# Modulation products summed in batches with one turn for each, and some of them moved to other places of the program

## The reference

```python
m_lat = jnp.split(s_lat @ w_ada[li] + b_ada[li], 6, axis=-1)     # s_lat = silu(c)
m_ctx = jnp.split(s_ctx @ w_ada[li] + b_ada[li], 6, axis=-1)
h = rms_norm(x, g_mix[li]) * (1.0 + m_lat[1]) + m_lat[0]
p = h @ w_in[li]                       # 9 x 256 columns: Fourier, attention, gMLP parts
...
x = x + m_lat[2] * (y @ w_out[li])
h = rms_norm(x, g_ffn[li]) * (1.0 + m_lat[4]) + m_lat[3]
x = x + m_lat[5] * conv_ffn(h, ffn_up[li], ffn_conv[li], ffn_conv_b[li], ffn_down[li])
```

## Time and profile before

| | |
|---|---|
| runs | 3271.11, 3277.59, 3277.39 us; median 3277.39 |
| profiled execution | 3273.77 us, of it the span of the trace 3272.0 us |
| PE busy | 3098.2 us (95%) |
| DVE, ACT, GpSimd busy | 1319.4, 742.9, 542.3 us |
| modulation chunks (line 229), PE busy | 114.0 us |
| loaded from HBM | 334.26 MB, 102 GB/s over the span |

### The profile page before, as it was taken

How to read it: one execution, slowest core, us unless ns; L and a number is a source line. 1 busy time by engine, 2 the same in 40 slices (tenths; PEclk the granted TensorE clock), 3 DMA queues, 4 the chain that set the end, 5 groups by cost and what they waited for, 6 DMA issues and landing times.

```text
span 3272.0 us, 39252 instructions
## 1 busy us (share of the span) xinstructions
PE 3098.2 (95%) x15593; PEld 2342.5 (72%) x15593; DVE 1319.4 (40%) x2198; ACT 742.9 (23%) x1413; POOL 542.3 (17%) x445
## 2 busy tenths in 40 slices
PE   7989999999989899999979999999999998999999
PEld 4546478888655788644469888844488887698888
DVE  1045368772224343255456656532245322223100
ACT  2034121110123231134234444421000001221100
POOL 1000035554100000000022222100145442011000
PEclk9989999999998999999989999999999998999999
DMA  6228412222316443334300000121222223211343
GB/s 238 77 77 319 183 65 90 91 91 90 103 64 252 148 154 141 141 130 166 142 7 14 14 14 14 46 90 65 77 78 88 80 90 107 90 40 43 148 144 116
DMA packets 51808, 337.66 MB, mean 103 GB/s; under 512 B 6304, under 2 KB 7968, under 8 KB 12608
## 3 DMA queue, kind: packets, MB, share of 16 engines
q1 hardware_dynamic: 47088, 323.05, 27.4%
q10 hardware_dynamic: 2976, 7.14, 0.6%
q0 software_dynamic: 1584, 5.21, 0.5%
HBM read 334.26 MB, written 1.11 MB: 102 GB/s over the span
## 4 chain that ended last, share of the span: by engine, by line
PE 83%; issue 9%; ACT 4%; DVE 2%; DVEq 0%; ACTq 0%; DMA 0%; POOL 0%; POOLq 0%
PE psum L208 29%; PE psum L2482 24%; PE psum L229 3%; PE psum L304 3%; PE psum L1425 3%; PE psum L1407 2%; PE psum L2051 2%; PE psum L371 2%; PE psum L242 1%; PE psum L1416 1%; ACT h_sb L887 1%; PE psum L398 1%; ACT arena L1680 1%; PE psum L1463 1%; PE psum L1486 1%
## 5 line engine op out<-in xcount | busy, mean ns | idle before, releaser
L208 PE MATMUL psum<-h_sb,ring 128*128 128x256 f32 (+1 forms) x2560 | 792.0, 470 | 16.5 <-ACT h_sb L887 16.4
L208 PEld LDWEIGHTS psum<-h_sb,ring 128*128 128x128 f32 x2560 | 484.9, 191 | 312.6 <-issue 266.3
L208 PE MATMUL psum<-arena,ring 128*128 128x256 f32 (+1 forms) x1504 | 418.1, 442 | 16.9 <-DVEq L716 7.5
L208 PEld LDWEIGHTS psum<-arena,ring 128*128 128x128 f32 x1504 | 291.9, 194 | 144.1 <-issue 92.5
L2482 PE MATMUL psum<-arena,ring 128*128 128x256 f32 x1168 | 267.4, 379 | 0.0
L2482 PEld LDWEIGHTS psum<-arena,ring 128*128 128x128 f32 x1168 | 221.9, 190 | 30.2
L2482 PE MATMUL psum<-h_sb,ring 128*128 128x256 f32 x912 | 216.6, 387 | 8.6 <-ACT h_sb L887 8.5
L2482 PE MATMUL psum<-arena,c 128*128 128x256 f32 x888 | 205.2, 379 | 1.8 <-DVE arena L2520 1.2
L1730 POOL TENSOR_TENSOR ring<-c,gates 128x512 f32<-128x512 f32 x32 | 32.6, 1041 | 1026.9 <-PE psum L208 797.2
L2482 PEld LDWEIGHTS psum<-h_sb,ring 128*128 128x128 f32 x912 | 174.2, 193 | 39.8 <-ACT h_sb L887 8.6
L2482 PEld LDWEIGHTS psum<-arena,c 128*128 128x128 f32 x888 | 168.5, 190 | 25.8 <-DVE arena L2520 2.0
(11 more groups left out here) (311 smaller groups left out, 4240.9 us busy)
## 6 DMA issues: line engine op xcount, KB each, us to landing
ring<-in_stream SPq DMA_DIRECT2D x302, 1024.0 KB, 4.8
arena<-decays SPq DMA_DIRECT2D x24, 256.0 KB, 3.6
x_sb<-in_x ACTq DMA_DIRECT2D x1, 2048.0 KB, 17.5
arena<-in_rpb POOLq DMA_DIRECT2D x32, 64.0 KB, 5.3
arena<-in_c POOLq DMA_DIRECT2D x1, 1120.0 KB, 7.9
x_sb<-in_ctx ACTq DMA_DIRECT2D x1, 1024.0 KB, 7.0
c<-in_c ACTq DMA_DIRECT2D x1, 1024.0 KB, 4.9
out<-x_sb POOLq DMA_DIRECT2D x1, 1024.0 KB, 5.0
```

The lines of the kernel that those rows point to most:

```text
L208: ins = pe.matmul(out_ap, lhs(k), rhs(k), start=first and k == 0, stop=last and k == nk - 1)
```

## The change

- **Batches.** `ADA_BATCHES` cuts the 96 chunks into nine batches of 4 to 16. The stationary operand is now a window of 32 columns in a wider `silu_w` (992 columns in all) whose place depends on the chunk's number q in its batch, so that its two rows land at 2q and 2q+1 of each group of 32. All chunks of a batch accumulate in the same 256 columns of bank 7; ACT copies once for a batch, behind its last chunk, and PE turns once, with a wider `sel`. A turn stands ahead of the first chunk of the next batch, or at the end of four parts (`TURNED_AT_END`).
- **Places.** Of the 40 chunks of attention 0, 16 go into the first projection (two behind each of its first eight chunks) and 2 into the gap behind layer 0's output projection (`gap1`). Attention 1 keeps 17; 4 go into the gap behind layer 0's feed-forward stage (`gap2`), 3 behind layer 1's output projection (`gap3`), 4 behind its feed-forward stage (`gap4`); the layer 2 projection keeps 20. `GAP_AHEAD` says how many of a gap's chunks stand ahead of the norm's products on PE. The stream follows.
- **ACT.** `act_norm` copies the batch that ends in a gap before its table load and Ln. It waits for the modulation only behind the Exp. In layers 2 and 3 the norm now stands ahead of the loads of constants.
- **Start.** ACT loads `c` alone first (16 KB), then `ident`, the rest of `vec`, `ones`, `x`. PE no longer waits for all of them. The first norm's squares are added on DVE, so PE has two sum products instead of eight, behind the eight chunks.
- **Others.** The gains of layer 1 are made in the feed-forward stage of layer 0, and its second item waits for them; the two sets of GpSimd's sum buffers are swapped, and its second chunk there waits for the fourth turn.

```diff
+QKV_TURNS = 8
+QKV_ADA = [3] * 4 + [2] * 4
+ADA_PARTS = _spans([("ada_first", MIX_ADA), ("ada_in1", 16), ("ada_next0", 22), ("gap1", 2), ("gap2", 4),
+                    ("ada_next1", 17), ("gap3", 3), ("gap4", 4), ("ada_last", sum(QKV_ADA))])
+GAP_AHEAD = {"gap1": 2, "gap2": 0, "gap3": 1, "gap4": 2}
+ADA_BATCHES = [(0, 8), (8, 24), (24, 36), (36, 48), (48, 52), (52, 62), (62, 72), (72, 84), (84, 96)]
+TURNED_AT_END = ("ada_first", "gap1", "gap3", "ada_last")
...
         def pe_ada(pe, name, i):
 
             n, a = ada_at(name, i)
-            if a == 0:
-                pe.wait_ge(S["silu_ready"], 1)
-            elif i > 0:
-                pe_turn(pe, a - 1)
+            batch, q, last = ada_batch(a)
+            if a > 0 and q == 0 and a not in [ADA_PARTS[part][1] for part in TURNED_AT_END]:
+                pe_turn(pe, batch - 1)
             arrived(pe, n)
             for half in range(2):
                 for j in range(4):
                     k = 4 * half + j
-                    ins = pe.matmul(bank(7)[32 * j:32 * (j + 1), 0:256], silu[:, a // (2 * ADA_CHUNKS), k, :],
-                                    w[:, n % RING, k, :], start=half == 0, stop=half == 1)
+                    ins = pe.matmul(bank(7)[32 * j:32 * (j + 1), 0:256],
+                                    silu[:, a // (2 * ADA_CHUNKS), k, ADA_ROWS - 2 - 2 * q:2 * ADA_ROWS - 2 - 2 * q],
+                                    w[:, n % RING, k, :], start=q == 0 and half == 0, stop=last and half == 1)
                 ins.then_inc(S["products"], 1)
...
+        def pe_ada_first(pe):
+            pe.wait_ge(S["silu_ready"], 1)
+            for i in range(MIX_ADA):
+                pe_ada(pe, "ada_first", i)
+            pe_norm_sums(pe, 0, TOK)
+            pe.wait_ge(S["silu_ready"], 2)
+            pe_turn(pe, 0)
...
         def pe_norm_sums(pe, k, cols):
 
-            added = KT + 2 * k - 1
+            gap = f"gap{k}"
+            if gap in ADA_PARTS:
+                for i in range(GAP_AHEAD[gap]):
+                    pe_ada(pe, gap, i)
+            added = 2 * k + 1
             pe.wait_ge(S["n_sq"], added)
...
+            if gap in ADA_PARTS:
+                for i in range(GAP_AHEAD[gap], ada_count(gap)):
+                    pe_ada(pe, gap, i)
+                if gap in TURNED_AT_END:
+                    pe_turn(pe, ada_batch(ADA_PARTS[gap][1] - 1)[0])
...
+                if li == 0 and c < IN1_CHUNKS - 1:
+                    for i in range(2):
+                        pe_ada(pe, "ada_in1", 2 * c + i)
...
-        def act_norm(act, use, l, part, norm=None, streams=2):
+        def act_norm(act, use, l, part, norm=None, streams=2, mods=None):
+            if f"gap{norm}" in ADA_PARTS:
+                act_ada_all(act, f"gap{norm}")
 
             if norm is not None:
                 act_log_exp_set(act)
                 act.wait_ge(S["n_sum"], norm + 1)
                 act_rsqrt(act, rinv[:, 0:streams * SEQ], bank(5)[:, 0:streams * SEQ], 1.0 / D).then_inc(S["n_rinv"], 1)
+            if mods is not None:
+                act.wait_ge(S["mods_ready"], mods)
...
-            act.dma_start(vec[:, :], t["vec"]).then_inc(S["loaded_vec"], 16)
+            act.dma_start(vec[:, 0:4 * KT], t["vec"][:, 0:4 * KT]).then_inc(S["loaded_c"], 16)
             act.dma_start(ident[:, :], t["ident"]).then_inc(S["loaded_vec"], 16)
+            act.dma_start(vec[:, 4 * KT:], t["vec"][:, 4 * KT:]).then_inc(S["loaded_vec"], 16)
             act.dma_start(ones[:, :], t["ones"]).then_inc(S["loaded_vec"], 16)
...
-            dve_squares(dve)
+            for kt in range(KT):
+                dve_square(dve, kt, 2)
...
+        b["act_norm"](act, 4, 2, 0, 4, mods=4)
         act.wait_ge(T["arena_free"], 1)
         act.dma_start(self.c2[:, 0:CD["end"]], t["c_delta"]).then_inc(T["loaded_c2"], 16)
...
-            act.wait_ge(S["mods_ready"], 4)
+            act.wait_ge(S["mods_ready"], 5)
+            b["act_norm"](act, 6, 3, 0, 6)
             act.wait_ge(T["arena_free"], 2)
```

More of the change, by code:

```diff
@@ L51, in _offsets, with _spans @@
     return out
+def _spans(counts):
+    at, out = 0, {}
+    for name, count in counts:
+        out[name] = (at, at + count)
+        at += count
+    return out
 VEC_SIZES = [("c", 4 * KT)]
@@ L173, in build_program, with ada_count @@
         sched = {}
+        def ada_count(name):
+            first, end = ADA_PARTS[name]
+            return end - first
         def plan(name, chunks, results):
@@ L209, in k_products, with in1_chunk, qkv_chunk, qkv_turn @@
             ins.then_inc(S["products"], 1)
+        def in1_chunk(li, c):
+            return sched[f"1in{li}"][0] + (3 * c if li == 0 else c)
+        def qkv_chunk(c):
+            return sched["2qkv"][0] + c + sum(QKV_ADA[:c // 2]) + c % 2
+        def qkv_turn(i):
+            return [i < sum(QKV_ADA[:j + 1]) for j in range(QKV_TURNS)].index(True)
         def ada_at(name, i):
             first, end = ADA_PARTS[name]
+            if name == "ada_in1":
+                return in1_chunk(0, i // 2) + 1 + i % 2, first + i
             if name == "ada_last":
-                return sched["2qkv"][0] + 5 * (i // 3) + (1, 3, 4)[i % 3], first + i
+                j = qkv_turn(i)
+                r = i - sum(QKV_ADA[:j])
+                return qkv_chunk(2 * j + (r > 0)) + 1 + (r > 1), first + i
             return sched[name][0] + i, first + i
@@ L236, in turned, with pe_turn @@
             return bank(7)[:, at + 2 * m0:at + 2 * m1]
-        def pe_turn(pe, a):
-            pe.wait_ge(S["ada_copied"], a + 1)
-            l, c = divmod(a, ADA_CHUNKS)
+        def pe_turn(pe, batch):
+            pe.wait_ge(S["ada_copied"], batch + 1)
+            first, end = ADA_BATCHES[batch]
+            l, c = divmod(first, ADA_CHUNKS)
+            cols = turned(l, 2 * c, 2 * (c + end - first)).rearrange("p (q m s) -> p m q s", m=2, s=2)
             for m in range(2):
-                ins = pe.matmul(turned(l, 2 * c + m, 2 * c + m + 1), rows[:, 256 * (a % 2) + 128 * m:256 * (a % 2) + 128 * (m + 1)],
-                                sel[:, :], start=True, stop=True)
+                at = 256 * (batch % 2) + 128 * m
+                ins = pe.matmul(cols[:, m], rows[:, at:at + 128],
+                                sel[:, 0:2 * (end - first)].rearrange("p (q s) -> p q s", s=2), start=True, stop=True)
             ins.then_inc(S["ada_turned"], 1)
-        def pe_ada_all(pe, name):
-            first, end = ADA_PARTS[name]
-            for i in range(end - first):
-                pe_ada(pe, name, i)
-            pe_turn(pe, end - 1)
+        def pe_ada_first(pe):
[5 more added lines that the diff above has]
+            pe_turn(pe, 0)
         def act_ada(act, name, i):
             n, a = ada_at(name, i)
+            batch, _, last = ada_batch(a)
+            if not last:
+                return
             act.wait_ge(S["products"], 2 * (n + 1))
-            if a >= 2:
-                act.wait_ge(S["ada_turned"], a - 1)
-            act.copy(rows[:, 256 * (a % 2):256 * (a % 2) + 256], bank(7)[:, 0:256]).then_inc(S["ada_copied"], 1)
+            if batch >= 2:
+                act.wait_ge(S["ada_turned"], batch - 1)
+            act.copy(rows[:, 256 * (batch % 2):256 * (batch % 2) + 256], bank(7)[:, 0:256]).then_inc(S["ada_copied"], 1)
         def act_ada_all(act, name):
@@ L1041, in _ @@
                 if li == 0:
[L1042 to L1046 removed]
+                    pe_ada_first(pe)
                 pe_in1(pe, li)
@@ L2723, in _constants2, with layout_second @@
                  for m in (tri + strict + pair, tri + span[0] + span[1], strict + pair))
-def layout_second(i, stream, out):
+def layout_second(i, stream, out, ada):
     dn = i["dn_w_in_2"][0]
-    qkv, ada = _chunks(dn[:, :4096]), _chunks(i["ada_w_2"][1])
-    for j in range(QKV_CHUNKS // 2):
-        stream.append(np.stack([qkv[2 * j], ada[3 * j], qkv[2 * j + 1], ada[3 * j + 1], ada[3 * j + 2]]))
+    qkv, ada = _chunks(dn[:, :4096]), ada[slice(*ADA_PARTS["ada_last"])]
+    for j in range(QKV_TURNS):
+        m = sum(QKV_ADA[:j])
+        stream.append(np.stack([qkv[2 * j], ada[m], qkv[2 * j + 1], *ada[m + 1:m + QKV_ADA[j]]]))
     stream.append(_chunks(dn[:, 4096:6144]))
```

140 lines of the change are left out of this document (70 added, 70 removed).

## The result

The changed kernel takes 3222.89 us (median of 4 runs, 3221.47 to 3224.05), the kernel before 3274.49 on the same chip (4 runs; the forecast started from the median of three of them, 3277.39). The ratio is 0.9842, with a 95% interval of 0.9825 to 0.9859: faster by 51.6 us, some eight times what a measurement can tell from no change. The forecast was 3221 with a range of 3207 to 3241. The profiled execution took 3221.47 us, its span 3219.6, against 3273.77 and 3272.0 before: -52.4 in the trace.

A forecast was written before the change was run, and what follows sets the result against it. TensorE (PE) was taken as the bound, 83% of the chain of waits. Ten terms summed to -56.4 us, giving 3217.4 profiled and a median of 3221; range 3207 to 3241, its own case 3212 to 3241 at 72%.

The forecast's parts named there:

- Start, -12.5: Kernel start: with one turn and the small c load first, chunk landings set the pace; -12.5 us, bounds -8 and -14.
- Attention 1, -19.5: Layer 1 attention: fewer chunks, turns and half-clock work, less some DVE lateness; -19.5 us, bounds -16 and -21.
- Attention 0, -36.5: Layer 0 attention: 40 chunks become 22 and 40 turns 2, DVE partly late; -36.5 us, bounds -33 and -39.
- the rule of the clock: Attention 0: the skill says recent PE busyness releases the throttle, a row disagrees; by the rule 1.7 us would not be there.
- Gap 1, +0.9: Behind layer 0's output projection: two chunks, 2.0 us, fill an idle of 1.17; +0.9 us, up to +2.
- Gap 2, +8.5: Behind layer 0's feed-forward stage: four chunks, copy and table load delay the norm's Ln; +8.5 us, from +5.7 to +9.4.
- Gap 3: Behind layer 1's output projection: copy and table load ahead of the Ln, two chunks behind the norm; +4.0 us, up to +6.
- Gap 4, 0: Behind layer 1's feed-forward stage: closes no batch, norm's ACT part now before four DMA issues; 0, bounds -1 and +1.
- Layer 2 projection, -14.7: Layer 2 projection: four chunks, 22 turns at 0.44 us and two copy waits of 0.5 go; -14.7 us.
- the softmax chain: Rival, 8%: in attention the softmax chain already sets the pace, so latent units stay at 4.07 us; 3248 us.
- the clock did come up: Rival, 4%: in attention the clock stays at 0.50 because PE has pauses in every unit; +110, 3331 us.
- the ring: Rival, 6%: in the first projection chunks come late because GpSimd's 3 MB of constants load too; +10, 3231 us.

The follow-up runs named there:

- no_moves: The changed kernel with all moved chunks back in attention and the layer 2 projection; batches, start and norm order kept: 3219.15 us, ratio 0.9830.
- The second profile: The changed kernel run once more, unedited: median 3225.02 us; this profile took 3228.22 us.
- late_chunks: The combined kernel with no chunk in the first six units of both attention stages, the same number spread over the others: 3215.12 us.
- combined kernel: The changed kernel with gap 1 emptied, copies of gaps 2 and 3 later, three gap 2 chunks ahead of the norm's sums, one behind: 3209.62 us.

## Why the prediction was right, and which steps were off

- *Start, -12.5.* The sum was right. What set it was the landings, as said, but x landed near 22.2 us (19.1 behind its issue) instead of 19.7, and the fourth chunk at 22; the eighth landed at 31 instead of 30. The squares and their adds, done near 31.7, stayed under it.
- *First projection, +16.0 (+16.5), GLA norm, -2.6 (-2.6).* Right in mechanism and size, the second shown by undoing it.
- *Attention 1, -19.5 (-19.6).* The chunks, the turns and a share for half clock (some -3.3 in the first units, where -2.3 was counted) came as forecast. That it fits to 0.1 is luck: the four products at the stage's end took 3.68 us, at half clock, where they had 1.98 before, and the output projection behind them then gained 1.2.
- *Attention 0, -36.5 (-34.5).* The price of a turn holds (0.41 where the turns came back). At the full-clock prices, 18 chunks at 1.00 and 38 turns at 0.52 on average, the stage would give 37.8; 3.3 of it did not come. The first units, up to the scores at 238.52 in the trace before, fell short by 0.6, where the sum counted another 1.2 won for the half clock: the mis-sized term. Behind the last transposes 1.1 is missing (one of the turns had stood inside a wait, and PE's waits for DVE are 0.6 longer), which the sum did not have. The other 1.6 are spread over the units, near the 1.7 counted for DVE. That 22 and 24 chunks take the same time is the clock at the stage's end, not DVE. (The prediction's passage on the rule of the clock puts its share at 1.7; the term in the sum is 1.2.)
- *Gap 1, +0.9 (+4.3): the step that failed.* It read "GpSimd's first weight sums now start behind the first of them and still end before PE's use". They did end before PE's use, but I weighed them against PE alone and not against DVE, which multiplies at the same time: 11.70 us instead of 5.98. The 0.9 itself was right; the 3.4 on top are the slower multiplications. Emptying the gap and moving GpSimd's second set both show it.
- *Gap 2, +8.5 (+5.9).* The mechanism was right (copy, table load, Ln behind the chunks); the term of the chunks was mis-sized, since they ran at nearly full clock, 4.30 us where I took nearly half clock. Gap 3 is 1.0 over its term and inside its bound; putting the copy behind the Exp gave 3.6 back.
- *Gap 4, 0 (+0.2).* Without its four chunks, no_moves is some 3 us shorter there, so the chunks cost 3 and something gave 3 back. The earlier norm, which the step names, is the likely cause; no run takes it away at this gap.
- *Layer 2 projection, -14.7 (-12.0).* Turns 22 x 0.41 = 9.0 and chunks 4.0 make 13.0. The turns' price was 0.44 in the sum, and the waits counted as gone (2 x 0.5) were not won: behind the last turn PE now idles for 1.74 us before the decay products at 1601.05. The profile names no releaser for that wait, and its cause stays open.
- *Not in the sum: -4.3 at the start of the delta rule and +1.6 in GLA.* Both move between executions of one program. The second profile gives the 4.3 back. The time from GLA's first product to the end is 497.41 before, 499.06 after, and 495.9 to 500.8 in the other traces.

So the forecast of 3221 against 3222.89 is closer than its steps. In the trace, -56.4 was forecast and -52.4 came. Gaps 1, 3 and 4 and the layer 2 projection gave 7.3 us less than summed, attention 0 2.0 less, and GLA took 1.6 more; gap 2 came out 2.6 better, and the first profile's luck with the clock in the delta rule hid 4.3. Another 2.2 of the distance went by chance of the medians: the forecast added 3.6 to the profiled time, and the measured median lies 1.4 above its own. (The bounds of the steps sum to -65.7 and -37.3, not to -65 and -36.) The rivals: the softmax chain did not set the pace in the earlier trace rows's units, only where chunks are taken away; the clock did come up; the gaps did cost; and the ring did not starve in the first projection, but would have in attention 0 had the chunks stayed there. The rule on the clock that was weighed against the earlier trace rows: in late_chunks PE was less busy in 230 to 240 than in the combined kernel and was granted the full clock earlier. In no_moves, with a chunk in every unit and PE busy for 4.00 of 4.00 us from 212 on, it came still earlier, 10.1 us behind the first scores. So how busy PE looks in the rows did not foretell it here either.

## What to carry to other kernels

When small chained steps are batched away, ask what they had been hiding: here a stage that was bound by PE came within reach of its loads, and the fix (moving work out of it) won nothing that could be measured. Work placed in a gap costs what it delays on every queue it touches: the copy on ACT ahead of a table load, the ring slots that the next stage's first load needs, and the engine (GpSimd) that it releases early into another engine's (DVE's) critical multiplications. Filling a gap with PE work is cheap when part of it stands ahead of the gap's chain and the copy behind it, as gap 2 of the combined kernel shows.

## What was not expected of the hardware

- DVE's 128x512 multiplication with both inputs in SBUF takes 0.68 us alone and 1.75 beside GpSimd's tensor_tensor; on 128x1024 it is 1.23 alone and 2.12 beside it, and GpSimd's own 128x512 goes from 1.27 to 1.53 or 2.06.
- One program, two profiles, 4.9 us apart in 27 us of work, because the granted clock stayed at 0.50 for 4 us or for over 12. Terms of this size in a chain with pauses can't be credited to an edit from one trace.
- The full clock came 2 to 3 us earlier in attention when the first units had no chunk (one trace). But it also came early in no_moves, where every unit had one: 10.1 us behind the first scores, against 13.3 in late_chunks and 16.6 to 17.1 in the eleven traces between.
- In the nine traces with 22 chunks in attention 0 the granted clock fell ahead of the stage's last four products (3.3 to 3.6 us); in the three with 24 it did not (1.98). So the two chunks did not make the stage longer.
